# Seven block products instead of eight in eight down-projection stages of a two-block transformer kernel

## What is computed

```
# first block: D_FF = 4096
x = x + jnp.square(jax.nn.relu(h @ w_ff1)) @ w_ff2

# second block, twice (l = 0, 1): D_FF_2 = 2816
up = xn @ w_up ; a, g = jnp.split(up, 2, axis=-1)
a = causal_dwconv(a, conv_w)              # three taps over the tokens
x = x + (jax.nn.silu(a) * g) @ w_down
```

## Time and profile before

| | |
|---|---|
| median of three runs | 2031.22 us |
| span of the profiled execution | 2029.2 us |
| time around the span (median less span) | 2.0 us |
| TensorE busy, matmuls | 2022.2 us, 10270 |
| VectorE busy | 993.0 us (49%) |
| ScalarE busy | 795.4 us (39%) |
| GpSimd busy | 870.7 us (43%) |
| DMA | 194 MB, 96 GB/s |

### The profile page before, as it was taken

How to read it: one execution, slowest core, us unless ns; L and a number is a source line. 1 busy time by engine, 2 the same in 40 slices (tenths; PEclk the granted TensorE clock), 3 DMA queues, 4 the chain that set the end, 5 groups by cost and what they waited for, 6 DMA issues and landing times.

```text
span 2029.2 us, 25410 instructions
## 1 busy us (share of the span) xinstructions
PE 2022.2 (100%) x10270; PEld 1659.3 (82%) x10270; DVE 993.0 (49%) x1502; ACT 795.4 (39%) x1144; POOL 870.7 (43%) x357
## 2 busy tenths in 40 slices
PE   9999999999999999999999999999999999999999
PEld 7888888888888888888888888888877778888887
DVE  4688888634221314434463242454377746334142
ACT  6455556534222224512432222246377743223222
POOL 4334443644444444444444444453422234444444
PEclk9999999999999999999999999999999999999999
DMA  5222222442333332323333333333311123323323
GB/s 179 83 84 74 84 84 84 130 134 94 104 94 104 94 94 94 104 94 91 96 94 104 94 94 104 94 115 93 96 61 57 59 76 94 104 91 98 100 93 114
DMA packets 55270, 194.38 MB, mean 96 GB/s; under 512 B 6129, under 2 KB 6641, under 8 KB 55153
## 3 DMA queue, kind: packets, MB, share of 16 engines
q1 hardware_dynamic: 55152, 192.75, 30.6%
HBM read 190.62 MB, written 2.10 MB: 95 GB/s over the span
## 4 chain that ended last, share of the span: by engine, by line
PE 98%; DVE 1%; DMA 0%; SPq 0%; issue 0%; ACT 0%; DVEq 0%
PE ps L1399 30%; PE ps L1400 30%; PE ps L1401 30%; PE ps L1766 1%; PE ps L1732 1%; PE ps L1757 1%; PE ps L1689 1%; PE ps L1691 1%; PE ps L1690 1%; PE ps L1539 1%; PE ps L1407 0%; PE ps L1437 0%; PE ps L1561 0%; DMA w_raw<-in_panels 0%; PE ps L1563 0%; PE ps L1548 0%
## 5 line engine op out<-in xcount | busy, mean ns | idle before, releaser
L355 POOL TENSOR_TENSOR w_lo<-w_raw,w_hi 128x1024 fp32r<-128x1024 f32 x353 | 870.5, 2469 | 1146.5 <-ACT w_hi L374 1118.8
L1399 PE MATMUL ps<-a_hi,w_hi 128*128 128x512 f32 x1472 | 580.9, 395 | 0.3 <-DVE x L848 0.2
L1401 PE MATMUL ps<-a_hi,w_lo 128*128 128x512 f32 x1472 | 573.6, 390 | 0.0
L1400 PE MATMUL ps<-a_lo,w_hi 128*128 128x512 f32 x1472 | 573.3, 389 | 0.0
L374 ACT CAST w_hi<-w_raw 128x1024 fp32r<-128x1024 f32 x353 | 366.0, 1041 | 326.2 <-PE ps L1401 289.5
L1399 PE MATMUL ps<-b_hi,w_hi 128*128 128x512 f32 x1176 | 458.5, 390 | 0.3 <-DVE x L848 0.2
L1401 PE MATMUL ps<-b_hi,w_lo 128*128 128x512 f32 x1176 | 457.6, 389 | 0.0
L1400 PE MATMUL ps<-b_lo,w_hi 128*128 128x512 f32 x1176 | 457.5, 389 | 0.0
L814 DVE TENSOR_TENSOR arena<-ps,inv_rms 128x512 f32<-128x512 f32 x200 | 138.0, 690 | 407.8 <-PE ps L1401 384.4
L1399 PEld LDWEIGHTS ps<-a_hi,w_hi 128*128 128x128 f32 x1472 | 276.3, 188 | 60.5 <-issue 2.8
L1400 PEld LDWEIGHTS ps<-a_lo,w_hi 128*128 128x128 f32 x1472 | 276.4, 188 | 58.1 <-issue 2.2
(11 more groups left out here) (208 smaller groups left out, 1622.7 us busy)
## 6 DMA issues: line engine op xcount, KB each, us to landing
w_raw<-in_panels SPq DMA_DIRECT2D x353, 512.0 KB, 3.5
x<-in_xT SPq DMA_DIRECT2D x16, 256.0 KB, 2.9
outT<-x SPq DMA_DIRECT2D x7, 256.0 KB, 3.8
consts<-in_const SPq DMA_DIRECT2D x1, 528.5 KB, 8.0
arena<-in_rows SPq DMA_DIRECT2D x1, 256.0 KB, 4.5
arena<-in_ws SPq DMA_DIRECT2D x1, 256.0 KB, 5.0
outT<-x SPq DMA_DIRECT2D x2, 128.0 KB, 1.8
consts<-in_late SPq DMA_DIRECT2D x1, 168.0 KB, 2.7
```

Source lines behind the costliest of these rows:

```text
L355: nc.gpsimd.tensor_tensor(w_lo[:, p % RING, :], w_raw[:, p % RING, :], w_hi[:, p % RING, :].bitcast(F), ALU.subtract).then_inc(w_low, 1)
L1399: nc.tensor.matmul(o, wh, hi[:, kt, :], start=(kt == 0), stop=False)
L1400: nc.tensor.matmul(o, wh, lo[:, kt, :], start=False, stop=False)
L1401: ins = nc.tensor.matmul(o, wl, hi[:, kt, :], start=False, stop=(kt == tiles - 1))
```

## The change

Eight of the eleven chunks have their down half rewritten: chunks 0 to 2 of the first network, chunks 0 and 1 of the second, and all three of the third (the last of them has 6 tiles, the others 8). Two panels (two output tiles) are now one pair, and the matrix product of a pair is cut in blocks: the weights into A11, A12 (first panel, first and second half of the inner tiles) and A21, A22 (second panel), the hidden tiles into B11, B12 (first half of the tiles, first and second 256 tokens) and B21, B22. The seven products of Strassen's method in Winograd's form are made in the order A11 B11, S1 T1, A12 B21, S4 B22, S2 T2, A22 T4, S3 T3, with

```diff
@@ SyncE
             def load(p):
                 if p >= RING:
                     sp.wait_ge(w_low, p - RING + 1)
+                    if PAIR_OF.get(p - RING, (0, 1))[1] == 0:
+                        sp.wait_ge(s_made, 4 * PAIR_OF[p - RING][0] + 4)
@@ GpSimd
+            def rest_low_of(ch, i):
+                key = ("ff1", ch)
+                pool.wait_ge(b1_high, B1_HIGH[key] + 4 + i + 1)
+                nc.gpsimd.tensor_tensor(a_lo[:, 4 + i, :], relu_sq[:, i % 2, :], a_hi[:, 4 + i, :].bitcast(F),
+                                        ALU.subtract).then_inc(rest_low, 1)
@@ ScalarE
             def high(p):
...
+                if PAIR_OF.get(p, (0, 0))[1] == 1:
+                    act.wait_ge(s_made, 4 * PAIR_OF[p][0] + 2)
...
+            def high_of_sum(q, i, h):
+                act.wait_ge(s_made, 4 * q + 4)
+                if q > 0:
+                    act.wait_ge(part_made, 7 * (q - 1) + S_AFTER[i])      # S_AFTER = (4, 5, 7)
+                split(s_hi[:, i, 0:h], ps[:, S_BANKS[i], 0:h]).then_inc(s_high, 1)
+            def down_pairs(key):
+                p0, tiles = down_stage(*key)
+                for j in range(DT // 2):
+                    p = p0 + 2 * j
+                    high(p + FEED)
+                    high(p + FEED + 1)
+                    if j < DT // 2 - 1:
+                        for i in range(3):
+                            high_of_sum(PAIR_AT[p + 2], i, tiles // 2 * P)
@@ VectorE
+            def sum_weights(q, tiles, part):
...
+                if part == 0:
...
+                    v.tensor_tensor(s3, a11, a21, ALU.subtract).then_inc(s_made, 1)
+                    dve.wait_ge(s_made, 4 * q + 1)
+                    v.tensor_tensor(a21, a21, a22, ALU.add).then_inc(s_made, 1)
+                else:
+                    dve.wait_ge(s_made, 4 * q + 2)
+                    v.tensor_tensor(s2, a21, a11, ALU.subtract).then_inc(s_made, 1)
+                    dve.wait_ge(s_made, 4 * q + 3)
+                    v.tensor_tensor(s4, a12, s2, ALU.subtract).then_inc(s_made, 1)
+            def down_pairs(key):
+                p0, tiles = down_stage(*key)
+                for j in range(DT // 2):
+                    q = PAIR_AT[p0 + 2 * j]
+                    more = j < DT // 2 - 1
+                    if j > 0:
+                        low_of_sum(q, 2, tiles)
+                        add_third(p0, j - 1)
+                    if more:
+                        sum_weights(q + 1, tiles, 0)
+                    if j > 0 or key[0] != "ff1":
+                        add_first(p0, j)
+                    if more:
+                        sum_weights(q + 1, tiles, 1)
+                    add_sides(p0, j)
+                    add_second(p0, j)
+                    if more:
+                        low_of_sum(q + 1, 0, tiles)
+                        low_of_sum(q + 1, 1, tiles)
+                    add_crossing(p0, j)
+                add_third(p0, DT // 2 - 1)
+            def ff1_up_folded(ch):
+                def finish(m):
...
+                    if m < 4:
+                        low_first(key, m, A)
+                        t1(key, m)
+                        low_t1(key, m, A)
+                        return
+                    dve.wait_ge(hid_raw, 8 * ch + m + 1)
+                    t2_t3(key, m - 4, raw, 4)
+                    t4(key, m - 4, raw, 4)
+                    low_t23(key, m - 4, 4)
+                    if m == 7:
+                        low_of_sum(q, 1, DT)
+                    low_t4(key, m - 4, raw, 4)
+                for m in range(DT):
...
+                    v.scalar_tensor_tensor(relu[:, m % 2, :], bank(p0 + m), 0.0, inv_rms[:, :],
+                                           ALU.max, ALU.mult).then_inc(evicted, 1)
+                    if m > 0:
+                        finish(m - 1)
+                    if m in (5, 6):
+                        sum_weights(q, DT, m - 5)
+                    if m == 6:
+                        low_of_sum(q, 0, DT)
+                add_first(p0 + DT, 0)
+                finish(7)
+                low_of_sum(q, 2, DT)
@@ VectorE, ffn(l), last tile of a folded chunk, between the convolution and the take-out of g
+                        if key in FOLDED and m == size - 1:
+                            q = PAIR_AT[p + 2]
+                            sum_weights(q, size, 0)
+                            sum_weights(q, size, 1)
+                            for i in range(3):
+                                low_of_sum(q, i, size)
@@ TensorE
+            def down_pairs(key, to):
...
+                for j in range(DT // 2):
...
+                    pe.wait_ge(w_low, p + 1)
+                    pe.wait_ge(evicted, p - (1 if j == 0 else 2))
+                    block(acc, a11, ...)
+                    pe.wait_ge(w_low, p + 2)
+                    pe.wait_ge(side_read, 2 * q)
+                    block(p5, s1, ...)
+                    block(p2, a12, ...)
+                    pe.wait_ge(s_low, 3 * q + 1)
+                    if j > 0:
+                        pe.wait_ge(evicted, p - 1)
+                    block(p3, s4, ...)
+                    pe.wait_ge(s_low, 3 * q + 2)
+                    pe.wait_ge(acc_read, 2 * q + 1)
+                    block(acc, s2, ...)
+                    block(p4, a22, ...)
+                    pe.wait_ge(s_low, 3 * q + 3)
+                    pe.wait_ge(acc_read, 2 * q + 2)
+                    block(acc, s3, ...)
```

More of the change, by code:

```diff
@@ L45, with down_stage @@
 N_PANELS = len(ORDER)
+HALF = SEQ // 2
+FOLDED = [("ff1", 0), ("ff1", 1), ("ff1", 2)] + [(f"ffn_{_l}", _n) for _l in range(2) for _n in range(3) if (_l, _n) != (0, 2)]
+def down_stage(name, n):
+    if name == "ff1":
+        return START["ff1"] + 16 * n + DT, DT
+    return START[name] + 2 * sum(FF2_CHUNKS[:n + 1]) + DT * n, FF2_CHUNKS[n]
+PAIR_AT, TILES_AT, PAIRS = {}, {}, []
+for _name, _n in FOLDED:
+    _p0, _tiles = down_stage(_name, _n)
+    for _m in range(0, DT, 2):
+        PAIR_AT[_p0 + _m] = len(PAIRS)
+        PAIRS.append(_p0 + _m)
+    TILES_AT[_name, _n] = _tiles
+PAIR_OF = {}
+for _p in PAIRS:
+    PAIR_OF[_p], PAIR_OF[_p + 1] = (PAIR_AT[_p], 0), (PAIR_AT[_p], 1)
+WHOLE = [sum(1 for _i in range(_p + 1) if _i not in PAIR_OF) for _p in range(N_PANELS)]
+B1_HIGH, T_HIGH, PART_LOW, REST_LOW = {}, {}, {}, {}
+_b = _t = _l = _r = 0
+for _key in FOLDED:
+    _k2 = TILES_AT[_key] // 2
+    B1_HIGH[_key], T_HIGH[_key], PART_LOW[_key], REST_LOW[_key] = _b, _t, _l, _r
+    _b, _t, _r = _b + 2 * _k2, _t + 3 * _k2, _r + _k2
+    _l += 4 * _k2
 LEVEL_GROUPS = ((0, 1), (2, 3), (4, 5), (6,))
@@ L182, in build @@
         gy = take(2, SEQ)
-        used[0] = after_y
+        used[0] = common + 8 * SEQ + 2 * (SEQ + 2)
+        keep = [take(SEQ), take(SEQ)]
         relu = take(2, SEQ)
         relu_sq = take(2, SEQ)
+        used[0] += 2 * SEQ
+        at_sums = used[0]
+        used[0] += 2 * 3 * SEQ + 2 * 4 * HALF
+        keep += [take(SEQ), take(SEQ)]
+        arena_space.close()
+        sb("below_t23", [P, common])
+        t23_hi, t23_lo = sb("t23_hi", [P, 4, SEQ], R), sb("t23_lo", [P, 4, SEQ], R)
+        sb("below_sums", [P, at_sums - common - 8 * SEQ])
+        s_hi, s_lo = sb("s_hi", [P, 3, SEQ], R), sb("s_lo", [P, 3, SEQ], R)
+        t4_hi, t4_lo = sb("t4_hi", [P, 4, HALF], R), sb("t4_lo", [P, 4, HALF], R)
+        sb("above_sums", [P, ARENA - used[0] + 2 * SEQ])
         used[0] = common
@@ L276, in bank_of, with wait_slot @@
             return p if p < GROUPS else p % 2
+        SIDE_BANKS = (2, 3)
+        S_BANKS = (6, 4, 5)
+        S_AFTER = (4, 5, 7)
+        def wait_slot(eng, p):
+            if p < RING:
+                return
+            if p - RING in PAIR_OF:
+                q, second = PAIR_OF[p - RING]
+                eng.wait_ge(part_made, 7 * q + (6 if second else 3))
+            else:
+                eng.wait_ge(made, WHOLE[p - RING])
         def even(buf):
@@ new lines, in low_of_sum, with low_first @@
+            def low_of_sum(q, i, tiles):
+                h = tiles // 2 * P
+                dve.wait_ge(s_high, 3 * q + i + 1)
+                v.tensor_tensor(s_lo[:, i, 0:h], ps[:, S_BANKS[i], 0:h], s_hi[:, i, 0:h].bitcast(F),
+                                ALU.subtract).then_inc(s_low, 1)
+            def low_first(key, m, to):
+                dve.wait_ge(b1_high, B1_HIGH[key] + m + 1)
+                v.tensor_tensor(to[1][:, m, 0:HALF], keep[m][:, 0:HALF], to[0][:, m, 0:HALF].bitcast(F),
+                                ALU.subtract).then_inc(part_low, 1)
@@ new lines, in add_third @@
+            def add_third(p0, j):
+                q, m = PAIR_AT[p0 + 2 * j], 2 * j
+                dve.wait_ge(part_made, 7 * q + 7)
+                dve.wait_ge(evicted, p0 + m + 1)
+                if p0 + m + 2 < N_PANELS:
+                    both = x[:, m + 1, :].rearrange("p (a n) -> p a n", a=2)
+                    v.tensor_tensor(both, both, acc_of(p0, j).unsqueeze(1).broadcast_to([P, 2, HALF]),
```

(5 more changed lines are left out.)

239 lines of the change are left out of this document (218 added, 21 removed).

## The result

The kernel after takes 2096.33 us in the median (2095.86 to 2096.91, four runs), the kernel before 2031.09 beside it: 1.0322 times as long, interval 1.0307 to 1.0336. The prediction was 2088 us, with a range of 2025 to 2118. Spans: 2095.1 against 2029.2 us.

A forecast was written before the change was run, and what follows sets the result against it. TensorE, busy 100% of the span, bounds the kernel before; afterwards VectorE's work and its lock with GpSimd delay it. Stage terms 24 + 22.5 + 10.4 = 57 us onto 2029.2, plus 2.0 around it, give 2088 us, range 2025 to 2118.

The forecast's parts named there:

- The lock: VectorE instructions reading only SBUF wait for GpSimd's to end, then take 0.55 us; sums into PSUM counted as blocked too.
- Middle pairs: Pairs between a stage's first and last: 10.24 us each instead of 10.88, 0.64 us saved instead of 1.36.
- The entry in the later networks: Start of down halves, other networks: 8-tile stages 49.1 against 43.5 us, in all +22.5; 6-tile stage +10.4.
- the walk: Step-by-step schedule of a stage's pairs; in later networks' pair 0, `add_second` ends at 17.75 and the pair at 19.15 us.
- The entry in the first network: Start of the down half in three stages: 50.5 or 52.6 against 43.5 us, taken as +8.0 each, +24.
- late case: First-network entry with S2 not ahead of GpSimd: first low part at 6.5 us, pair 0 ends at 22.6, stage 52.6.
- The matmul: A 256-column matmul in the changed stages takes 113.3 ns, half of 226.7; bounds 109 and 121.
- TensorE's term: Matmuls of the eight changed stages: 337.3 us falls to 295, 42 us less (22 to 53), if always fed.
- Rival 3: Worse than the walk: matmuls at 121 ns, and TensorE pauses that may drop its clock to 1.2 GHz; 2121 us; chance 0.11.
- Rivals 1 and 2: 1: lock hardly bites, 2027 us, chance 0.14. 2: TensorE alone counts, 1989 up to 2011 us, chance 0.09.

The follow-up runs named there:

- the first experiment: Kernel after, with three memsets in a row replacing GpSimd's subtraction for the changed stages' down panels: 2049.92 us, ratio 1.0092.
- Two edits: Against the kernel after: pair 0's adds ahead of the next sums, 2077.43 us; ScalarE's next-panel cast only after S3 and S1, 2074.09 us; both, 2082.65 us.

## Why the prediction was right, and where its sizes were off

**The account.** Stages 337.3 us before, 404 after. TensorE's own matmuls went to 2604 x 119.0 ns = 309.9: -27. The remaining 94 us are 72 in which TensorE starts nothing and some 20 in which its matmuls take 213 ns instead of 119. Two runs price the causes. Without GpSimd's reads of the panels the stages took 357.7: 46 us less. With VectorE's added work one column wide they took 328.4, that is 76 us less than 404; GpSimd's reads are still there in this run, so it isn't a step on top of the first, and the 29 us between the two are a difference of two runs and not a term that was taken out alone. The last 18.5 (to 309.9) are S1's way over cast and GpSimd at the entry, 10 us of waiting and 8 of half clock behind it. Another order of taking away would share them out otherwise, since the waits cover each other.

**The lock** was the mechanism, and the first experiment shows it as such. The rule behind it, in the Trainium skill, "SBUF — State Buffer", section "Who interferes with whom", goes by the inputs: two in SBUF, against a GpSimd instruction that reads SBUF. It leaves open sums that write PSUM. The trace agrees with it, and decides those as the prediction had counted them: S3 2.7 us in the median.

**Middle pairs** were put at 10.24 and took 10.37; the last pair of a stage 9.52 and 9.98. Both differences are the matmul, below.

**The entry in the later networks** came out nearly step by step (predicted, then the timeline): S1's low part 5.7 and 5.8, the last tile's low part 9.2 and 9.0, T parts 10.8 and 10.4, S1 of the next pair 14.4 and 13.9, product 5 at 14.8 and 14.3. Then the walk went wrong by one step: it let product 7 wait for `add_second` till 17.75, but that had ended at 17.0, and product 7 followed product 6 at 17.2. Pair 0 took 18.6 instead of 19.15, the longer matmuls of the other pairs gave that back, and the stage took 49.3 for 49.1. That the stage came out so close is luck in this part: two errors of more than half a microsecond cancelled. The last stage took 43.4 for 43.0.

**The entry in the first network** is the term that was sized too low: +8.0 a stage, measured +10.4 to +11.3. All three stages fell into the prediction's late case, where S2 comes in behind GpSimd: tile 7 is taken out at 6.1 (said: 6.5). After that product 5 started at 13.3, released by S2's low part (said: 11.9, in the late case some 2.1 more), and product 7 at 20.5 (said: 19.1, in the late case 21.2). So both came a little ahead of the late case, but product 7 took 2.7 us and not 1.36: TensorE had stood still for 4 us, and the clock had fallen. Busy time in three stretches of one such stage, which began at 624.28:

```profile
641.00:645.00 4.00, 0.24 (x1) 0.27 (x2) 3.82 (x7) 2.13 (x3) 2.14 (x1) 0.83 0.17 34
645.00:648.00 3.00, 3.00 (x15) 3.00 (x16) 1.41 (x3) 0.24 (x1) 0.22 (x1) 0.50 0.83 277
650.00:679.00 29.00, 28.89 (x241) 28.70 (x240) 20.91 (x31) 9.59 (x12) 13.75 (x6) 0.99 0.31 96
```

TensorE is idle from 641 to nearly 645, then at a granted clock of 0.50 up to 650.5, 3 us into pair 1, then at full speed. Pair 0 took 23.2 for the late case's 22.6, pair 1 10.4 to 11.3 for 10.24, the stages 54.4 for 52.6 in the mean. Over three stages the term came out 8.6 us too low (32.6 for 24): 3.3 for the middle taken between two cases, and 5.3 for the half clock in pairs 0 and 1 and the longer matmuls (0.13 in a middle pair, 0.46 in the last). That is the 8 us by which the forecast fell short.

**The matmul** was mis-sized: 113.3 ns, measured 119.0 where the clock is full. A 512-column one takes 226.7, so both take their columns at 2.4 GHz (213 and 107) and 12 to 13 ns more. At the half clock the 256 columns take 213 ns and nothing more, so such a matmul costs 1.8 times the 119 and not twice as much. The bound of 121 was made in just this way and was the better value; the twin rows that spoke for less are matmuls on half the rows. TensorE's term was -27, not -42. This is the largest error in a single term of the prediction, and it hardly shows in the total, because where VectorE sets the time a longer matmul is hidden.

**Rival 3's mechanism** took place: twelve stretches of 1.2 GHz inside the changed stages, 54.6 us in all, none before. Its price, 24 us beside the longer matmuls, was too high here: 187 slow matmuls cost 94 ns more each, 18 us, and most of them ran ahead of waits for VectorE. By the run with dummy matmuls some 6 us of it counted: 1.3 a stage for product 7 in the first network, the rest in pair 1 behind it and in the stage with 6 tiles. The price isn't small by itself: in the run with one column, where VectorE covers nothing, 15 slow matmuls cost 1.6 us in each of five stages.

**Rivals 1 and 2** are out: no lock means 2050 here, not 2027. Half of the 23 us are the longer matmul, which is not hidden there (24 pairs behind the first ones of 10.0 instead of 9.52, or 7.5 instead of 7.14: 11 us), the other half is pair 0, where VectorE's own queue is longer than that sum had it. And TensorE alone counts only when VectorE's added work is nearly nothing, which gave 2018, not 1989 to 2011 (2009 by its own 22 us), as nobody had S1's way over ScalarE and GpSimd, and the clock behind that wait, in the account.

## What to carry to other kernels

Before trading matmuls for sums, add up what the sums put on VectorE between two points at which TensorE waits, and charge each one that reads only SBUF with GpSimd's whole instruction where the two can meet; here a saving of 27 us on TensorE brought 94 us of waits and slow matmuls. Count a halved matmul at half its columns plus its full fixed part (12 to 13 ns here). Look at the entry of a stage first: with 8 tiles the middle pairs were even faster than before (10.4 against 10.9 us), and the loss came from the first pair, where the sums stood in front of the work that the next product needed. And before an instruction is moved forward, follow its result through every engine that hands it on: S1 made earlier was of no use, because its cast kept its place in ScalarE's order.

## What was not expected of the hardware

- What the half clock costs depends on where it falls. Ahead of a wait for another engine it was hidden (three stages with 15 to 23 slow matmuls and without any: 49.3 us both times); behind the last wait the same stretch cost 1.6 us a stage. In the run with one column it followed a pause of 2 us.
- Two edits that each gained 19 and 22 us gave 14 together, since a wait on one engine's result inherits the place of that result in its queue.
- VectorE's sum with two inputs in SBUF and its output in PSUM is blocked as long (2.7 us) as the one that stays in SBUF (2.8), and memsets of GpSimd into `w_lo` block neither (0.70 at most).
- GpSimd's low part of half a panel's width takes 1.30 us in the median, of a whole one 2.40: nearly all of it goes by the columns.
